# A two-layer decoder trunk on one core: layers written out, output projections and norms tile by tile, whole weight units, router with tokens as rows

## The chip, the cores and the metric

The kernel runs on one core of a Trainium2 chip, in one launch. The metric is device time in microseconds. A core has five engines with their own instruction streams, which meet only at semaphores: TensorE (PE; its weight loads are PEld), VectorE (DVE), ScalarE (ACT), GpSimd (POOL) and SyncE (SP). Here SP issues the weight loads and the output, POOL the other transfers.

## The reference, cut to what matters

One sequence of 256 tokens, width 1024, runs through two layers of three pre-norm residual parts. All tensors are float32.

```python
for layer in range(2):
    x = x + hybrid_mixer(rmsnorm(x, mix_norm_g[layer]), w_in, conv_w, pool_w, pool_scale, w_out, rel_bias)
    x = x + memory_cross_attention(rmsnorm(x, xattn_norm_g[layer]), mem_n, wq_x, wkv_x, wo_x)
    hn = rmsnorm(x, ffn_norm_g[layer])
    if layer == 0:                       # silu(hn @ w1) * (hn @ w3) @ w2, inner width 2816
        x = x + swiglu(hn, w13_dense, w2_dense)
    else:                                # top 2 of 8 experts, inner width 3584
        x = x + moe_swiglu(hn, router_w, w13_moe, w2_moe)
return rmsnorm(x, final_norm_g)
```

The mixer projects to 2560 columns: q, k, v of eight heads of 64, an input u of a causal pooling mixer (windows 2 to 16, mean less the token, then a small matrix per group), and b, c, h of a gated convolution of width 3 (b * conv(c * h)). The attention has a bias by distance, a 33-row table times a 0/1 matrix. Results of the three are joined and projected by w_out. Cross-attention has four heads of 128 over 256 memory tokens, whose norm is shared by both layers.

## The kernel before, in words

**Weights.** The host cuts all large weights into units of 128 x 2048 floats (1 MB), in the order of use, some of them half units (the projection wo_x, the last 256 columns of the dense stage). SP loads them in that order into a ring `raw` of six (`load`, L316). Each is split in two parts whose products PE can do in one pass each: ACT copies it to `w_hi` in a shorter format (`hi`, L460, in two halves; `hi_whole`, L468, for the expert items), DVE subtracts to get `w_lo` (`lo`, L707; `lo_whole`, L714). There are three slots of w_hi and w_lo. Activations are split in the same way (`xT_hi`, `xT_lo`; `yT_hi`, `yT_lo`). Each product is three matmuls (`passes`, L1104: high by high, high by low, low by high). `tokens_out` gives 128 tokens as rows, 512 columns at a time, for both row tiles t of 128 tokens; `features_out` gives features as rows, 256 tokens at a time. PE counts used halves in `unit_used`, DVE freed raw halves in `raw_free`; ACT, DVE, PE and SP wait on such counts.

**A norm** (`norm` on ACT L474, DVE L725, PE L1143): DVE squares and sums tile 0 while ACT does tile 1; ACT takes ln and exp(-ln/2) as a guess, DVE improves it by one Newton step, then scales both tiles with the gain row; PE transposes 16 blocks of 128 x 128 in four groups, and each group goes through ACT (`turned_hi`) and DVE (`turned_lo`). Between a projection and its norm stands `add_to_x` (L754), which adds the four 128 x 512 banks to x; the norm starts when all four are in.

**The order** of every engine's stream is written by hand. PE: the norm of x; the table product for the bias; then a hardware loop over two layers. In a layer: units 0 to 3 (q, k), 4 and 5 (v; in layer 0 the memory's norm between them), then ten iterations of attention (L1176 to 1208): iteration i does logits of head i, transposes of head i-1, values of head i-2, and in the first four also half a unit of features_out (units 6, 7). DVE adds the bias, takes the maximum and copies the transposes (L820 to 859), with units 8 to 10 split and the pooling in between; ACT does the exponentials. After it: unit 8, transposes of the attention's result, the pool matrices, unit 9, the output projection (units 10 to 13), memory keys (14, 15), norm, queries (17, 18) and memory values (16, 19), cross-attention (L1239 to 1273), projection by four half units, norm. Layer 0 goes on into the dense stage: five steps in a hardware loop and a rest of half width, with banks 4 to 7 cleared by four matmuls with zeros. Both loops, and the conditions on l, are run-time control flow on all engines.

**The bias table.** DVE copies the product's eight rows; POOL sends each row to memory 128 times (`skew`, L386), waits for it, and reads it back with one element less per partition, which lines up the distances (L399). DVE waits for that before the first head. The mem tile lies in the same buffer until its norm is done.

**The router** (L1345 to 1377): 16 matmuls with the router as stationary part give logits with experts as rows; a copy, two transposes and two steps on DVE turn and add them. DVE picks the top two, PE ranks the tokens of each expert, DVE builds a 0/1 matrix S, and PE gathers the first expert's rows by it. Then come the items, one for each expert, 42 units each (a hardware loop), and some for an overfull expert if any. At the end four indirect transfers bring the rows back, DVE adds them in, and the final norm follows.

The matmuls' waits on the low part of x at the start of a layer:

```python
            pe.wait_ge(sem("xT_lo"), l * 16 + 3)
            features_out(st, 0, 0, xs, (4, 5), True, False)
            pe.wait_ge(sem("xT_lo"), l * 16 + 4)
            features_out(st, 1, 4, xs, (4, 5), False, True)
```

## Time and profile before

| | |
|---|---|
| median of 3 runs (lowest, highest) | 1610.94 us (1609.52, 1611.62) |
| the profiled execution: its time / its span | 1611.02 us / 1609.1 us |
| mean granted TensorE clock | 0.962 |
| PE / PEld busy | 1499.7 / 1262.4 us |
| DVE / ACT / POOL busy | 1191.5 / 961.4 / 38.5 us |
| expert items, first to last matmul | about 633 to 1583 us |
| HBM read / written | 456.36 / 17.30 MB |

The profile is of one execution. Its span runs from the first to the last instruction. Busy time of PE says that matmuls were under way, not that they ran at full rate: the granted clock is 1.00 or 0.50 (2.4 or 1.2 GHz). Idle time is put down to what released the waiting engine.

### The profile page before, as it was taken

The page shows a single profiled execution, that of the slowest core. Times are in us where ns is not written, and L with a number is a line of the kernel's source. Part 1 is how long each engine was busy: PE and PEld are TensorE (multiplying, and loading weights), DVE is VectorE, ACT ScalarE, POOL GpSimd, SP SyncE. Part 2 cuts the span into 40 slices and gives each one's busy share as a digit, 9 for nine tenths or more (in the row PEclk, how much of TensorE's full clock was granted, in tenths as well). Part 3 has the DMA queues.
Part 4 walks back from the last instruction along what each step waited for, and adds up shares of the span by engine and source line. Part 5 has one row for each costly group of instructions (what it writes and reads, how often), then busy time and mean ns, then how long its engine had stood idle before and what let it go on. Part 6 is the DMA issues. An engine that isn't in the chain of part 4 may idle for free.

```text
span 1609.1 us, 22211 instructions
## 1 busy us (share of the span) xinstructions
PE 1499.7 (93%) x7397; PEld 1262.4 (78%) x7398; DVE 1191.5 (74%) x1027; ACT 961.4 (60%) x876; POOL 38.5 (2%) x53
## 2 busy tenths in 40 slices
PE   7699879999698986999999999999999999999993
PEld 6588767888687965888888888888888888888882
DVE  5467445454547646888888988898888888988884
ACT  4334334353334434777777777777777777777772
POOL 1000000000000000100000000000000000000001
PEclk9889989999898997999999999999999999999997
DMA  9524735435432422999999999999999999999992
GB/s 350 190 105 171 297 134 198 168 141 209 159 136 82 157 116 99 413 404 371 385 368 393 381 367 392 380 374 389 372 374 393 374 373 392 376 372 395 370 360 106
DMA packets 69723, 466.04 MB, mean 290 GB/s; under 512 B 7998, under 2 KB 8014, under 8 KB 17697
## 3 DMA queue, kind: packets, MB, share of 16 engines
q1 hardware_dynamic: 61328, 435.97, 69.9%
q0 software_dynamic: 8336, 29.34, 5.3%
q8 instruction: 31, 0.51, 0.1%
q14 instruction: 28, 0.22, 0.0%
HBM read 456.36 MB, written 17.30 MB: 294 GB/s over the span
## 4 chain that ended last, share of the span: by engine, by line
PE 89%; DMA 4%; DVE 4%; issue 2%; ACT 1%; DVEq 0%; POOLq 0%; POOL 0%; ACTq 0%
PE bank L1107 28%; PE bank L1109 27%; PE bank L1108 27%; DMA skew<-prob 3%; PE bank L1392 2%; PE bank L1149 1%; DMA bias<-skew 1%; PE bank L1381 0%; DVE xn L746 0%; PE bank L1271 0%; DVE w_lo L711 0%; PE bank L1371 0%; DMA probT<-done,row_i 0%; DVE w_lo L717 0%; PE bank L1251 0%
## 5 line engine op out<-in xcount | busy, mean ns | idle before, releaser
L717 DVE TENSOR_TENSOR w_lo<-raw,w_hi 128x2048 fp32r<-128x2048 f32 x336 | 769.0, 2292 | 103.1 <-ACT w_hi L471 99.9
L471 ACT ACTIVATE w_hi<-raw 128x2048 fp32r<-128x2048 f32 x336 | 642.9, 1916 | 126.3 <-PE bank L1109 126.3
L1107 PE MATMUL bank<-w_hi,yT_hi 128*128 128x512 f32 x1528 | 603.5, 395 | 6.4 <-DVE yT_lo L723 6.4
L1109 PE MATMUL bank<-w_hi,yT_lo 128*128 128x512 f32 x1528 | 596.8, 391 | 0.0
L1108 PE MATMUL bank<-w_lo,yT_hi 128*128 128x512 f32 x1528 | 595.9, 390 | 0.0
L1107 PEld LDWEIGHTS bank<-w_hi,yT_hi 128*128 128x128 f32 x1528 | 287.6, 188 | 66.9 <-issue 5.8
L1109 PEld LDWEIGHTS bank<-w_hi,yT_lo 128*128 128x128 f32 x1528 | 287.5, 188 | 61.0
L1108 PEld LDWEIGHTS bank<-w_lo,yT_hi 128*128 128x128 f32 x1528 | 288.0, 188 | 58.0
L711 DVE TENSOR_TENSOR w_lo<-raw,w_hi 128x1024 fp32r<-128x1024 f32 (+1 forms) x168 | 182.1, 1131 | 83.3 <-ACT w_hi L465 82.0
L465 ACT ACTIVATE w_hi<-raw 128x1024 fp32r<-128x1024 f32 (+1 forms) x168 | 155.8, 986 | 85.7 <-PE bank L1109 80.8
L723 DVE TENSOR_TENSOR yT_lo<-bank,yT_hi 128x512 fp32r<-128x512 f32 (+1 forms) x94 | 62.3, 678 | 59.1 <-ACT yT_hi L499 53.5
L1107 PE MATMUL bank<-xT_hi,w_hi 128*128 128x256 f32 x320 | 96.3, 301 | 6.9 <-DVE w_lo L711 6.9
L1108 PE MATMUL bank<-xT_lo,w_hi 128*128 128x256 f32 x320 | 94.5, 295 | 0.0
L1109 PE MATMUL bank<-xT_hi,w_lo 128*128 128x256 f32 x320 | 94.2, 294 | 0.0
L1107 PE MATMUL bank<-w_hi,xT_hi 128*128 128x512 f32 (+1 forms) x224 | 86.4, 386 | 6.9 <-DVE w_lo L711 6.8
L1109 PE MATMUL bank<-w_hi,xT_lo 128*128 128x512 f32 (+1 forms) x224 | 85.4, 381 | 0.0
L1108 PE MATMUL bank<-w_lo,xT_hi 128*128 128x512 f32 (+1 forms) x224 | 85.3, 381 | 0.0
L493 ACT ACTIVATE qk<-bank 128x512 f32<-128x512 f32 (+1 forms) x68 | 39.7, 592 | 75.8 <-PE bank L1109 75.8
L1107 PEld LDWEIGHTS bank<-xT_hi,w_hi 128*128 128x128 f32 x320 | 65.8, 206 | 10.2 <-DVE w_lo L711 8.7
L658 ACT ACTIVATE yT_hi<-bank 128x512 fp32r<-128x512 f32 x56 | 33.5, 599 | 59.2 <-PE bank L1392 59.2
L1108 PEld LDWEIGHTS bank<-xT_lo,w_hi 128*128 128x128 f32 x320 | 65.8, 206 | 0.1
L1109 PEld LDWEIGHTS bank<-xT_hi,w_lo 128*128 128x128 f32 x320 | 65.5, 205 | 0.0
(220 smaller groups left out, 919.4 us busy)
## 6 DMA issues: line engine op xcount, KB each, us to landing
raw<-in_moe_units SPq DMA_DIRECT2D x336, 1024.0 KB, 7.1
raw<-in_layer_units SPq DMA_DIRECT2D x40, 1024.0 KB, 6.7
raw<-in_dense_units SPq DMA_DIRECT2D x30, 1024.0 KB, 4.9
sent<-in_x POOLq DMA_DIRECT2D x1, 6144.0 KB, 33.3
xn<-sent POOLq DMA_DIRECT2D x9, 512.0 KB, 8.0
raw<-in_wo_units SPq DMA_DIRECT2D x8, 512.0 KB, 3.4
done<-qk POOLq DMA_DIRECT2D x8, 512.0 KB, 8.8
raw<-in_dense_halves SPq DMA_DIRECT2D x6, 512.0 KB, 3.2
```

The source lines that it names most:

```text
L465: act.activation(w_hi[:, u % SPLIT, half, 0:n], raw[:, u % RAW, half * n:(half + 1) * n], ACT.Copy)\
L471: act.activation(w_hi[:, u % SPLIT, :, :].rearrange("p a n -> p (a n)"), raw[:, u % RAW, :], ACT.Copy)\
L493: act.activation(hid[:, t, 0:width], bank[g_bank + t][:, 0:width], ACT.Silu)\
L658: act.activation(hT_hi[j % 2], banks4(3), ACT.Copy).then_inc(sem("hidT_hi"), 1)
L711: dve.tensor_tensor(w_lo[:, u % SPLIT, half, 0:n], raw[:, u % RAW, half * n:(half + 1) * n], w_hi[:, u % SPLIT, half, 0:n].bitcast(F32), A ...
L717: dve.tensor_tensor(w_lo[:, u % SPLIT, :, :].rearrange("p a n -> p (a n)"), raw[:, u % RAW, :], w_hi[:, u % SPLIT, :, :].rearrange("p a n ...
L723: return dve.tensor_tensor(out, src, hi_part.bitcast(F32), ALU.subtract)
L1107: pe.matmul(out, hi_l, hi_r, start=start, stop=False, skip_group_check=True)
L1108: pe.matmul(out, hi_l, lo_r, start=False, stop=False, skip_group_check=True)
L1109: return pe.matmul(out, lo_l, hi_r, start=False, stop=stop, skip_group_check=True)
L1149: mm = pe.transpose(bank[banks[2 * t + half]][:, k * P:(k + 1) * P], xn[:, t, a:a + P], ident)
L1392: mm = pe.transpose(bank[3][:, k * P:(k + 1) * P], hid[:, 0, k * P:(k + 1) * P], ident)
```

## The change

- Loops over the layers and over the dense steps are written out in Python: every engine's stream is straight code up to the items. `Stream` counts slots from an offset, so that a layer may have any number of units.
- All units are whole: 22 in a layer and 33 in the dense stage instead of 24 and 36. wo_x is two units, the dense rest three.
- The order of the input columns is v, q, k, (u, c), (h, b). The last seven halves of units 6 to 9 stand inside attention's iterations 0 to 6. u and c are copied by ACT to own buffers after head 2; pooling on DVE moves to iterations 3 and 4, the pool matrices to iteration 7. The output projection begins with its upper half (pooling, then convolution).
- Norms go tile by tile and half by half: ACT does all squares (two of 512 a tile), its `guess` and DVE's `root` are per tile. `project` finishes t0's sums before t1's; `norm_of_sum` on ACT and DVE works on t0 meanwhile, with splitting of the next units in between; `tile_by_tile` begins the next stage with t0.
- The dense stage's last units are ordered in the same way; the clearing matmuls go.
- In cross-attention the memory values' second unit (19) runs in iterations 0 and 1.
- x comes in two transfers, only the identity of `mats` from SP at the start. The skew table has 32 copies of a row instead of 128; SP issues it after unit 5, waits for it, and issues four reads of 32 partitions, then goes on with unit 6. The memory lies in qk's buffer.
- Router: x's parts are the stationary side, 16 matmuls for each tile, t0's before t1 is turned; the result has tokens as rows, and one reduction adds the parts.
- At the end rows come back tile by tile, and the final norm is per tile.

```diff
+LAYER_UNITS = 22
+DENSE_UNITS = 33
 ITEM_UNITS = 6 * (FE // FT)
 DENSE_STEPS = FD // FT
...
+    out += [unit(w_out, k, 4, c * 512, 512) for c, k in ((0, 4), (1, 4), (0, 0), (1, 0))]
     out += [unit(wkv, 4 * m, 4, 0, 512) for m in range(2)]
...
+                if l == 0 and u == RAW - 1:
+                    sp.wait_ge(sem("skew_rows"), 1)
+                    sp.dma_start(skew.ap(), skew_rows.unsqueeze(1).broadcast_to([HEADS, SKEW_P, SKEW_W]))\
+                        .then_inc(sem("skew_out"), 16)
+                    sp.wait_ge(sem("skew_out"), 16)
+                    for a in range(0, P, SKEW_P):
+                        sp.dma_start(bias[a:a + SKEW_P, :, :],
+                                     bass.AP(skew, P - 1 - a, [[SKEW_W - 1, SKEW_P], [SKEW_P * SKEW_W, HEADS], [1, T]]))\
+                            .then_inc(sem("bias_in"), 16)
...
-        pool.dma_start(skew.ap(), skew_rows.unsqueeze(1).broadcast_to([HEADS, P, SKEW_W])).then_inc(sem("skew_out"), 16)
...
+        def squares_of_sum(m, n, t, half):
+            act.wait_ge(sem("x_part"), 4 * n + 2 * t + half + 1)
+            square(m, t, half, x_tiles)
...
+        def guess(m, t):
+            act.wait_ge(sem("square"), 4 * m + 2 * t + 2)
+            act.wait_ge(sem("half_mean"), NT * m + t + 1)
+            act.activation(lnv[:, t:t + 1], ss[:, t, 1:2], ACT.Ln, scale=1.0 / D, bias=half_mean[:, t:t + 1])\
+                .then_inc(sem("ln_act"), 1)
+            act.wait_ge(sem("ln_act"), NT * m + t + 1)
+            act.activation(r0[:, t:t + 1], lnv[:, t:t + 1], ACT.Exp, scale=-0.5).then_inc(sem("rstd_guess"), 1)
...
+        def norm_of_sum(m, n, banks, st, u):
+            squares_of_sum(m, n, 0, 0)
+            squares_of_sum(m, n, 0, 1)
+            guess(m, 0)
+            hi(st, u, which=(0,))
+            squares_of_sum(m, n, 1, 0)
+            turned_hi(m, 0, banks[0:2], xT_hi)
+            hi(st, u, which=(1,))
+            squares_of_sum(m, n, 1, 1)
+            guess(m, 1)
+            hi(st, u + 1)
+            turned_hi(m, 1, banks[2:4], xT_hi)
...
+        def root(m, t):
+            a = slice(t, t + 1)
+            dve.wait_ge(sem("square"), 4 * m + 2 * t + 2)
+            dve.wait_ge(sem("half_mean"), NT * m + t + 1)
+            c.step(dve.tensor_scalar(mean[:, a], ss[:, t, 1:2], 1.0 / D, half_mean[:, a], ALU.mult, ALU.add))
+            dve.wait_ge(sem("rstd_guess"), NT * m + t + 1)
+            c.wait()
+            c.link(dve.scalar_tensor_tensor(newton[:, a], mean[:, a], r0[:, a], r0[:, a], ALU.mult, ALU.mult))
+            c.link(dve.tensor_scalar(newton[:, a], newton[:, a], -0.5, 1.5, ALU.mult, ALU.add))
+            c.link(dve.tensor_tensor(rstd[:, a], r0[:, a], newton[:, a], ALU.mult))
+        def scaled(m, t, src):
+            dve.wait_ge(sem("gain_in" if m else "first_gain_in"), 16 * m if m else 16)
+            for half in range(2):
+                s = slice(half * 512, (half + 1) * 512)
+                dve.scalar_tensor_tensor(xn[:, t, s], src[t][:, s], rstd[:, t:t + 1], g_row[:, s],
+                                         ALU.mult, ALU.mult).then_inc(sem("xn_ready"), 1)
...
+        def norm_of_sum(m, before, sums, banks, last, u, st):
+            dve.wait_ge(sem("sum_mm"), before + 1)
+            add_part(0, 0, sums[0])
+            half_means(m, 0)
+            dve.wait_ge(sem("sum_mm"), before + 2)
+            add_part(0, 1, sums[2])
+            root(m, 0)
+            scaled(m, 0, x_tiles)
+            if last[0] is None:
+                dve.wait_ge(sem("sum_mm"), before + 3)
             else:
...
+                used(dve, st, last[0])
+            add_part(1, 0, sums[1])
+            half_means(m, 1)
+            turned_lo(m, 0, banks[0:2], xT_hi, xT_lo)
+            used(dve, st, last[1])
+            add_part(1, 1, sums[3])
+            lo(st, u)
+            root(m, 1)
+            scaled(m, 1, x_tiles)
+            turned_lo(m, 1, banks[2:4], xT_hi, xT_lo)
+            lo(st, u + 1)
...
+                elif i == 3:
+                    dve.wait_ge(sem("u_sb"), l1)
+                    c.link(dve.tensor_tensor(B, U, pool_u[:, :, 1:T + 1], ALU.add))
...
                     c.link(dve.tensor_tensor(A[:, 1, :], B[:, 1, :], back(pool_b, 2)[:, 1, :], ALU.add))
...
+        def project(st, u, m, xs, sums, norm_banks):
             for t in range(NT):
...
+                for col in range(2):
+                    banks = sums[2 * col:2 * col + 2]
+                    first = u == 20
+                    if t == 0:
+                        tokens_out(st, u + col, 4, 512, xs, banks, first, True, tiles=(t,), count=False)\
+                            .then_inc(sem("sum_mm"), 1)
+                    elif col == 0:
+                        tokens_out(st, u, 4, 512, xs, banks, first, True, tiles=(t,))
+                    else:
+                        tokens_out(st, u + 1, 4, 512, xs, banks, first, True, which=(0,), tiles=(t,))
+                        turn_tile(m, 0, norm_banks[0:2])
+                        tokens_out(st, u + 1, 4, 512, xs, banks, first, True, which=(1,), tiles=(t,))
...
+        def tile_by_tile(st, u, m, banks, norm_banks):
+            lower, upper = (xT_hi, xT_lo, 0), (xT_hi, xT_lo, 4)
+            turned(m, 0, 0)
+            tokens_out(st, u, 4, 512, lower, banks, True, False, tiles=(0,), count=False)
+            turned(m, 0, 1)
+            tokens_out(st, u + 1, 4, 512, upper, banks, False, True, which=(0,), tiles=(0,), count=False)
+            if m:
+                turn_tile(m, 1, norm_banks[2:4])
+            tokens_out(st, u + 1, 4, 512, upper, banks, False, True, which=(1,), tiles=(0,), count=False)
+            turned(m, 1, 0)
+            tokens_out(st, u, 4, 512, lower, banks, True, False, tiles=(1,))
+            turned(m, 1, 1)
+            tokens_out(st, u + 1, 4, 512, upper, banks, False, True, tiles=(1,))
         pe.sem_inc(sem("unit_used"), 2 * SPLIT)
...
+            tile_by_tile(st, 0, 4 * l, (0, 1), (0, 1, 2, 3))
+            features_out(st, 2, 0, xs, (4, 5), True, False)
+            features_out(st, 3, 4, xs, (4, 5), False, True)
+            if l < 1:
+                pe.wait_ge(sem("skew_rows"), 1)
+                turn_tile(1, 0, (2, 3))
...
+                if i == 3:
+                    pe.wait_ge(sem("u_sb"), l1)
+                    pe.wait_ge(sem("c_sb"), l1)
+                if i < 7:
+                    u = 6 + (i + 1) // 2
+                    features_out(st, u, 4 * (u % 2), xs, (2, 3), u % 2 == 0, u % 2 == 1, which=((i + 1) % 2,))
+                if i == 7:
...
+            pe.wait_ge(sem("pool_lo"), l1 * 2)
+            tokens_out(st, 10, 4, 512, (yT_hi, yT_lo, 4), (0, 1), True, False, which=(0,))
+            tokens_out(st, 11, 4, 512, (yT_hi, yT_lo, 4), (6, 7), True, False, which=(0,))
             for t in range(NT):
                 pe.wait_ge(sem("y_tok"), l * 2 + t + 1)
                 for k in range(4):
                     mm = pe.transpose(bank[4 + t][:, k * P:(k + 1) * P], y_tok[:, t, k * P:(k + 1) * P], ident)
                 mm.then_inc(sem("yTok_mm"), 1)
...
+            pe.wait_ge(sem("conv_lo"), l1)
+            tokens_out(st, 10, 4, 512, (yT_hi, yT_lo, 4), (0, 1), False, False, which=(1,))
+            tokens_out(st, 11, 4, 512, (yT_hi, yT_lo, 4), (6, 7), False, False, which=(1,))
+            pe.wait_ge(sem("attn_lo"), l1 * NT)
+            m = 3 * l + 2
+            project(st, 12, m, (yT_hi, yT_lo, 0), (0, 1, 6, 7), (2, 3, 4, 5))
             ms = (memT_hi, memT_lo)
...
                 turn(FT // 2, NT)
+                down(st, e + 3, 1, tiles=(0,), count=False)
                 pe.wait_ge(sem("hidT_lo"), (DENSE_STEPS + 1) * NT)
...
+                down_short(st, e + 4, 0, 0)
+                down_short(st, e + 4, 0, 1)
+                down(st, e + 3, 1, tiles=(1,))
+                down_short(st, e + 4, 1, 0)
+                turn_tile(4, 0, (0, 1))
+                down_short(st, e + 4, 1, 1)
+        m = 3 * DEPTH
...
+        for t in range(NT):
+            turned(m, t, 1)
+            for k in range(KD):
+                for part in (xT_hi, xT_lo):
+                    mm = pe.matmul(bank[0][:, t * 2 * NE:(t + 1) * 2 * NE], part[:, k, t * P:(t + 1) * P],
+                                   router_parts[:, k, :], start=(k == 0 and part is xT_hi),
+                                   stop=(k == KD - 1 and part is xT_lo))
+            if t == 0:
+                turn_tile(m, 1, (6, 7))
         mm.then_inc(sem("router_mm"), 1)
```

## Rows read from the trace of the kernel before

**Rows 1.** The page, busy time of each engine (share of the span).

```profile
PE 1499.7 (93%) x7397; PEld 1262.4 (78%) x7398; DVE 1191.5 (74%) x1027; ACT 961.4 (60%) x876; POOL 38.5 (2%) x53
```

**Rows 2.** Windows: length; busy us of PE, PEld, DVE, ACT, POOL; granted clock, DMA share, GB/s.

```profile
0.00:633.00 633.00, 549.86 (x3077) 477.73 (x3078) 337.93 (x523) 249.69 (x394) 16.80 (x28) 0.92 0.47 172
...
633.00:1583.00 950.00, 949.81 (x4320) 784.64 (x4320) 843.98 (x493) 707.68 (x475) 17.31 (x20) 1.00 0.96 372
```

**Rows 3.** Waits of PE before 700 us: who waits for whom, total us, times, longest.

```profile
PE bank L1149 <- DVE xn L746: 27.5, 4, 9.9
PE bank L1197 <- ACT prob L533: 18.0, 8, 12.1
PE bank L1107 <- DVE w_lo L711: 13.8, 4, 5.2
PE bank L1107 <- DVE yT_lo L723: 6.4, 4, 1.8
PE bank L1352 <- issue: 4.6, 1, 4.6
PE bank L1260 <- ACT prob L580: 3.6, 4, 1.2
```

**Rows 4.** Timeline at the start: start us, us, instruction, [idle before <- releaser].

```profile
16.70 0.58 PE L1107 MATMUL bank<-xT_hi,w_hi 128*128 128x256 f32 x1 [1.77 <-DVE w_lo L711]
```

**Rows 5.** First attention transpose (timeline); DMA issues: count, KB, us to landing.

```profile
72.73 0.69 PE L1197 MATMUL bank<-mats,prob 128*128 128x128 f32 x2 [12.11 <-ACT prob L533]
...
skew<-prob POOLq DMA_DIRECT2D x1, 1536.0 KB, 40.4
...
bias<-skew POOLq DMA_DIRECT2D x1, 1024.0 KB, 14.0
```

**Rows 6.** Timeline of PE, attention of layer 1: heads 3, 4, 5, and the last.

```profile
477.12 0.49 PE L1185 MATMUL bank<-qk 64*128 64x128 f32 x2
...
482.00 0.48 PE L1185 MATMUL bank<-qk 64*128 64x128 f32 x2
...
483.94 0.48 PE L1185 MATMUL bank<-qk 64*128 64x128 f32 x2
...
498.41 0.63 PE L1205 MATMUL bank<-v,probT 128*128 128x64 f32 x2
```

**Rows 7.** Windows at the lower clock.

```profile
72.70:76.70 4.00, 3.97 (x19) 3.97 (x20) 0.56 (x1) 2.80 (x6) 0.00 (x0) 0.50 0.03 8
...
218.30:223.60 5.30, 5.30 (x13) 4.19 (x14) 5.30 (x5) 3.38 (x4) 0.00 (x0) 0.50 0.59 193
428.60:431.80 3.20, 3.20 (x15) 3.20 (x16) 3.20 (x3) 3.20 (x4) 0.00 (x0) 0.50 0.26 41
...
498.80:503.50 4.70, 4.70 (x24) 4.70 (x24) 2.37 (x4) 0.00 (x0) 0.00 (x0) 0.50 0.51 185
```

**Rows 8.** Windows over three norms, the last with the router.

```profile
205.20:218.30 13.10, 3.32 (x17) 3.09 (x17) 9.81 (x17) 7.62 (x12) 0.58 (x1) 0.81 0.13 41
413.10:428.60 15.50, 3.69 (x17) 3.27 (x16) 11.12 (x19) 6.40 (x11) 2.84 (x4) 0.66 0.16 43
600.20:633.20 33.00, 15.65 (x78) 13.39 (x77) 21.20 (x47) 12.36 (x16) 0.53 (x1) 0.64 0.32 113
```

**Rows 9.** The page, the splitting of half units: count, busy us, mean ns, idle before.

```profile
L711 DVE TENSOR_TENSOR w_lo<-raw,w_hi 128x1024 fp32r<-128x1024 f32 (+1 forms) x168 | 182.1, 1131 | 83.3 <-ACT w_hi L465 82.0
L465 ACT ACTIVATE w_hi<-raw 128x1024 fp32r<-128x1024 f32 (+1 forms) x168 | 155.8, 986 | 85.7 <-PE bank L1109 80.8
```

**Rows 10.** Timeline of DVE, norm before the dense stage: adding halves, scaling tiles.

```profile
205.20 1.29 DVE L762 TENSOR_TENSOR x<-x,bank 128x512 f32<-128x512 f32 x2 [4.15 <-PE bank L1109]
...
209.29 2.48 DVE L746 SCALAR_TENSOR_TENSOR xn<-x,rstd,g_row 128x1024 f32<-128x1024 f32 x2
```

**Rows 11.** DMA queues, instruction fetches: in 245:400 (a loop), 433:600 (straight code).

```profile
q8 instruction: 3, 0.05, 0.1%
...
q8 instruction: 8, 0.13, 0.3%
```

More of the change, by code:

```diff
@@ L572, in _ @@
[L572 to L574 removed]
+            hi(st, 20)
+            if l == DEPTH - 1:
+                act.wait_ge(sem("router_in"), 32)
+                act.activation(router_parts[:, :, 0:NE], router[:, :, :], ACT.Copy).then_inc(sem("router_hi"), 1)
             for h in range(XHEADS):
@@ L1341, in _ @@
                 pe.wait_ge(sem("hidT_lo"), (DENSE_STEPS + 1) * NT)
-                down(st, e + 6, NT, short=True, last=True)
-                norm(4, (0, 1, 2, 3))
-            pe.nop()
-        pe.wait_ge(sem("xT_lo"), 16 * DEPTH - 4)
-        pe.wait_ge(sem("router_lo"), 1)
-        for k in range(KD):
-            for part in (xT_hi, xT_lo):
-                mm = pe.matmul(bank[0][0:2 * NE, 0:T], router_parts[:, k, :], part[:, k, :],
-                               start=(k == 0 and part is xT_hi), stop=(k == KD - 1 and part is xT_lo))
```

784 lines of the change are left out of this document (360 added, 424 removed).

## The prediction, on record before the changed kernel was run

> **What bounds the kernel now.** I read the page first. PE is busy 93% of the span [rows 1], so gains can only come from the rest and from low clock. The windows split that: from 633 to 1583 us, the expert items, PE is busy 949.8 of 950 us at clock 1.00; before it, 549.9 of 633 us at clock 0.92 [rows 2]. The diff leaves the item loop alone (only slot numbers shift, as it starts at unit 77 instead of 84), and DMA, though at share 0.96, never makes PE wait there. So everything hangs on the first 633 us and the 26 us behind the items. The list of PE's waits names the places [rows 3]: transposes wait for the scaled rows of a norm (27.5 us in 4), attention transposes for the exponentials (18.0, of which 12.1 in one), first matmuls of a stage for w_lo (13.8) or for the low part of the activations (6.4). The windows on the lower clock show a second price behind each [rows 7]: half speed for 3 to 5 us after work resumes. A microsecond of full-speed PE work done at clock 0.50 costs a second one.
>
> **The change part by part.** The matmuls are the same in number and shape nearly everywhere, so I work with removed and added gaps. All durations are of the one profiled execution: span 1609.1 us, its time 1611.02, 0.1 above the median 1610.94.
>
> *1. Start.* The first matmul is at 16.70 us [rows 4]. x now comes in two tiles, and unit 0 is split before the second tile is turned. By my count ACT and DVE are still in the way: the squares of a tile are now two on ACT, and both tiles' scaling stands ahead of the first w_lo. First matmul at about 14.7, but at half speed at first. I take 1.5 us of gain; between 0 and 4.
>
> *2. Bias table.* PE stands 12.11 us before the first attention transpose [rows 5]: the skewed table took 40.4 us out and 14.0 us back. Then 4 us run at clock 0.50 [rows 7], costing 2. Now 32 copies of each row go out instead of 128: a quarter of 1536 KB, so at the old rate 10 us. Its source is still 8 partitions. It is issued by SP behind unit 5 once DVE has copied the rows, which now stands behind the splitting of units 0 and 1, about 20.4 us. Behind the six megabytes already in SP's queue it starts near 25 (1 MB passes in 2.8 us at 372 GB/s [rows 2]), ends near 35; the bias follows in four parts, at most the old 14: 49. Attention wants it at about 57 (72.7 less 12.1, less the 1.5 of step 1, less the head's own 2 us). So the wait goes, with its clock loss: 14.1. While SP waits for the skew table it issues no weights: unit 6 is asked for at about 36 and lands by 41 to 52; PE reaches it at about 55. Bounds 0 and 14.1.
>
> Here a rule speaks against the change. In rows 5 the table on its own queue took 40.4 us next to the weights. The Trainium skill (DMA: Bandwidth & Descriptors, Queues, rings and completion order) says that on each DMA engine the descriptors of a ring are consumed in order, while different rings are served in turn. By it the table no longer shares with the weights but waits for all six. That is the start at 25 used above, against 20.4 without the rule; the step keeps 8 us of slack either way, less in rival A.
>
> *3. Attention.* Iterations with half a unit of projection beside them last 4.88 us, those without 1.94 [rows 6]. In the old order only four of ten have filler. From 483.94 (head 5) to the end at about 498.8 the work is three iterations of 1.94 and the tails of two (1.1, 0.7), 7.6 us; it took 14.9. Lost 7.3, and 4.7 us at clock 0.50 behind it cost 2.3 more [rows 7]. That is 9.6; the waits for ACT prob beyond the 12.1, 5.9 us, lie about evenly in both layers, so I take 8.7 for layer 0 (less of it at the lower clock): together 18.3. Now iterations 0 to 6 have filler, and pool matmuls stand in the seventh. DVE per iteration: about 1.6 us of softmax and copy, and 2 x 1.13 for a unit [rows 9] or some 3 for pooling: inside 4.88. New: before the upper half of the output projection PE waits for the convolution (products, y_tok, taps, half of unit 12, its low part, some 7.7 us of DVE against 5.4 + 0.9 of PE): 1.4 us, once a layer. Net 18.3 - 3.0 = 15.3; bounds 8 and 18.
>
> *4. Norm behind the mixer's projection.* It was hidden behind the memory keys (no wait of it in the list). It stays behind them, but DVE now has one more chain: add, half unit pair, root, scaling before the second tile turns, 5.3 us against 5.7 of PE. I charge 1.0; bounds 0 and 4 of loss.
>
> *5. Cross-attention.* Unit 19 (values) moves into its first two iterations. The exponential's wait, 3.6 us in 4 [rows 3], loses its two longer parts: 2.4. Splitting of w_lo leaves the path between y_tok and the projection: 0.5 a layer. 3.4; bounds 0 and 5.
>
> *6. Norm before the dense stage.* From the last projection matmul to the first of the dense stage: 13.1 us [rows 8], then 5.3 us at 0.50, 2.7 lost [rows 7]. New order: with t0's sum 5.4 us ahead of t1's, its chain (add 0.65, two scalings of half a tile 1.3 [rows 10], and between them the square, logarithm, exponential and root, which the old order does in 2.8 from add to scaling for both tiles and I put at 2.4: 4.4) ends when PE has 1.4 us of projection left. Counting on from there: transposes 1.8, a wait of 0.3 for the scaling, 0.7 for the first low part, 1.0 for the second tile's scaling, which stands behind both halves of a w_lo: 3.8 in all instead of 15.8. Gain 12.0; bounds 7 and 13. The 2.5 us wait near 246 stays; the four clearing matmuls that go were inside it.
>
> *7. Layer boundary.* 15.5 us [rows 8], 3.2 us at 0.50 behind it (1.6) [rows 7], and 1.3 of the waits for yT_lo, which the last full down unit now covers. t1 follows t0 by two short and one full pass, so the new cost is again about 3.6. Gain 14.8; bounds 9 and 15.
>
> *8. Norm and router.* 33.0 us from the end of the projection to the first item [rows 8]. 4.6 of it PE waits for nothing the profile shows [rows 3]; about 2.9 of that lie after the last operand is ready. New: t0's 16 router matmuls run while t1 is normed; logits come out with tokens as rows, so a copy, two transposes and a copy (2.2 us) go. With the old stretch's durations, all inside those 33.0: end of projection to last xT_lo 8.1 + the interleaved transposes' 1.1, router 1.8, top-2 2.8, ranks 2.2, S 0.9, gather 5.6, its split 1.5: 24.0, and 0.5 for the hand-overs. Gain 8.5; bounds 4 (32 small matmuls, each with a full weight load, at half clock) and 12.
>
> *9. Tail.* The final norm runs on the same engines as the one of rows 10. Tile by tile, the squares of t1 now stand behind the root of t0 on ACT, whose half mean stands behind all four combinings on DVE. The second tile ends 0.3 later. -0.3; bounds -1 and 1.
>
> *10. Allowance.* New short waits stand close together at each norm; the clock dropped in such places before. Three windows of 3.4 us at half rate: -5. Bounds 0 and -10.
>
> Sum: 1.5 + 14.1 + 15.3 - 1.0 + 3.4 + 12.0 + 14.8 + 8.5 - 0.3 - 5.0 = 63.3 us. Span 1545.8, time 1547.7, less the 0.1: **1547.6 us**.
>
> **Rivals.**
> *A. The skew table blocks the weights.* If on SP's queue it still needs about 40 us (few source partitions), bias lands near 75 and unit 6 behind it: step 2 turns from +14.1 to -13. Saving 36, 1575 us. For: 40.4 us in rows 5. Against: a quarter of the bytes, and weights no longer beside it. 0.12.
> *B. Per-tile norms are longer than counted.* Each is a chain over three engines with single-column steps, and sits behind w_lo work in DVE's order. If each of the three big norms exposes 5 us more, and the convolution wait is 3 instead of 1.4: 1547.6 + 15 + 3 = 1566. For: rows 8, where 13 us were exposed. Against: nothing in the count is longer than its row. 0.15.
> *C. Instruction supply (ends slower).* Written-out layers and dense steps are straight code: PE's fetches in the dense stretch were 3 in a loop against 8 in as long a stretch of straight code [rows 11]. If a fetch stalled PE as at the router (2.9 us), 22 stalls eat the gain; with 25 or more, time is above 1611, say 1620. Against: those 8 fetches left no such wait in rows 3. 0.03.
> *D. More than counted.* Loop ends may cost beyond the router's. The Trainium skill (Runtime: NRT & Kernel Launch, Instruction fetch mechanics) says that a taken branch to code outside the fetched window stalls. By it the dense loop's turns would each pay, and writing it out would bring some 2.9 us at each of four turns, about 1536 us. This trace disagrees inside the loop: no wait there but 2.5 us for w_lo. 0.07.
>
> **How the numbers follow.** Forecast 0.63, own range 1536 to 1560; A 0.12, B 0.15, C 0.03, D 0.07. Range 1534 to 1574 holds the forecast, B, D and the nearer part of A. A change under 0.2% (3.2 us) can't be told from none here. All but C are faster by far more: faster 0.96, same 0.01, slower 0.03.
>
> **What would show it.** Right: no wait of ten us for ACT prob in layer 0; bias landed before 50 us; norm waits under 2 us each; items beginning near 570 instead of 633 and again 950 us long. Wrong: a DVE wait for the bias, PE waits on "issue", a clock of 0.50 in long stretches of the layers, or a longer item loop.

## The result, and the profile after

The changed kernel takes 1546.81 us (median of 4 runs, 1543.76 to 1548.75), the kernel before 1611.22 (4 runs, 1609.52 to 1611.62): ratio 0.96, 95% interval 0.9581 to 0.962. Forecast: 1547.6. The profiled execution took 1543.76 us, its span is 1541.9, 67.2 less than before; the forecast had 63.3 less.

The page's first rows of the kernel after stand beside [rows 1]; the clock's row shows one dip in 40 slices, the last slice aside.

```profile
PE 1479.3 (96%) x7408; PEld 1244.0 (81%) x7408; DVE 1187.9 (77%) x1052; ACT 973.6 (63%) x928; POOL 35.8 (2%) x53
...
PEclk9999999999999979999999999999999999999996
```

Windows of the kernel after, columns as in [rows 2]: what lies ahead of the items, then the items.

```profile
0.00:564.00 564.00, 529.24 (x3088) 459.18 (x3088) 334.43 (x543) 259.89 (x438) 15.61 (x28) 0.98 0.52 191
564.00:1514.00 950.00, 949.77 (x4320) 784.79 (x4320) 843.94 (x493) 707.77 (x475) 15.82 (x20) 1.00 0.96 372
```

The items are as long as before, 950 us. Everything was won ahead of them: 633 us became 564, with 20.6 us less of PE busy time (549.9 against 529.2) because less of it ran at half clock (0.92 to 0.98), and 48 us less idle. The end behind the items gave 1.5 us back. Waits of PE before 640 us in the kernel after, to be read against [rows 3]:

```profile
PE bank L1190 <- DVE xn L774: 14.0, 5, 9.4
PE bank L1147 <- DVE yT_lo L750: 5.1, 5, 1.5
PE bank L1147 <- DVE w_lo L738: 4.9, 4, 3.5
PE bank L1448 <- DVE mask L1043: 2.9, 1, 2.9
PE bank L1440 <- DVE xT_lo L750: 2.5, 2, 1.4
```

Of the 14.0 us for scaled rows 9.4 are the first wait of the kernel, for x; the four later ones together are 4.6, where there were 17.6 behind the first 9.9. Attention's waits for ACT prob, 18.0 in [rows 3], left this list; 0.4 us for the convolution stands there instead, in each layer. Timelines of the kernel after at its norms (start, length, instruction, idle before it): ahead of the dense stage, then at the layer boundary.

```profile
183.84 1.32 PE L1190 MATMUL bank<-mats,xn 128*128 128x128 f32 x8 [0.70 <-DVE xn L774]
...
372.81 1.32 PE L1190 MATMUL bank<-mats,xn 128*128 128x128 f32 x8 [0.69 <-DVE xn L774]
376.04 0.50 PE L1147 MATMUL bank<-w_hi,xT_hi 128*128 128x512 f32 x1 [0.52 <-DVE xT_lo L750]
```

Where 13.1 and 15.5 us stood [rows 8] there are pauses of 0.4 to 0.7 us. What is left above 2 us behind the start, by the timeline of PE, is one wait in the dense stage and two in the router:

```profile
206.34 0.73 PE L1147 MATMUL bank<-w_hi,xT_hi 128*128 128x512 f32 x1 [3.47 <-DVE w_lo L738]
...
543.41 1.97 PE L1190 MATMUL bank<-mats,xn 128*128 128x128 f32 x8 [2.47 <-DVE xn L774]
...
553.31 0.57 PE L1448 MATMUL bank<-mask,mats 128*128 128x8 f32 x2 [2.94 <-DVE mask L1043]
```

The low clock went with the waits, except here. Windows of the kernel after, against [rows 7] (which show a part of what there was: 99 us at 0.50 before the items, now 24):

```profile
206.40:209.80 3.40, 3.40 (x8) 2.71 (x9) 3.20 (x3) 1.37 (x2) 0.00 (x0) 0.50 0.26 43
...
540.90:561.40 20.50, 12.63 (x57) 12.03 (x57) 10.55 (x33) 5.05 (x7) 0.53 (x1) 0.50 0.34 128
```

### The profile page after: what moved, and what is told of

The parts are those of the page before. It is cut to its first block, busy times and chain, and to the rows that moved or that the text cites. A ratio compares the mean times of both kernels' runs of the same rounds, so it can differ in the third digit from the quotient of the medians.

```text
span 1541.9 us, 21452 instructions
## 1 busy us (share of the span) xinstructions
PE 1479.3 (96%) x7408; PEld 1244.0 (81%) x7408; DVE 1187.9 (77%) x1052; ACT 973.6 (63%) x928; POOL 35.8 (2%) x53
## 4 chain that ended last, share of the span: by engine, by line
PE 91%; DVE 5%; issue 1%; ACT 1%; DMA 1%; POOLq 0%; POOL 0%; ACTq 0%; DVEq 0%; SPq 0%
PE bank L1147 28%; PE bank L1149 28%; PE bank L1148 28%; PE bank L1479 2%; DVE w_lo L738 1%; DVE xn L774 1%; PE bank L1190 1%; PE bank L1264 0%; PE bank L1331 0%; PE bank L1274 0%; DMA g_row<-in_mix_norm_g 0%; PE bank L1262 0%; PE bank L1468 0%; PE bank L1351 0%; PE bank L1458 0%
## 5 line engine op out<-in xcount | busy, mean ns | idle before, releaser
L738 DVE TENSOR_TENSOR w_lo<-raw,w_hi 128x1024 fp32r<-128x1024 f32 x160 | 188.4, 1220 | 56.4 <-ACT w_hi L468 54.8
L468 ACT ACTIVATE w_hi<-raw 128x1024 fp32r<-128x1024 f32 x160 | 160.5, 1055 | 39.5 <-PE bank L1149 37.3
L1147 PE MATMUL bank<-xT_hi,w_hi 128*128 128x256 f32 x320 | 91.8, 287 | 0.0
L1148 PE MATMUL bank<-xT_lo,w_hi 128*128 128x256 f32 x320 | 90.5, 283 | 0.0
L1149 PE MATMUL bank<-xT_hi,w_lo 128*128 128x256 f32 x320 | 90.4, 283 | 0.0
L682 ACT ACTIVATE yT_hi<-bank 128x512 fp32r<-128x512 f32 x56 | 33.6, 599 | 59.3 <-PE bank L1479 59.3
L1147 PEld LDWEIGHTS bank<-xT_hi,w_hi 128*128 128x128 f32 x320 | 61.3, 192 | 0.7 <-DVE w_lo L738 0.7
L1148 PEld LDWEIGHTS bank<-xT_lo,w_hi 128*128 128x128 f32 x320 | 61.3, 192 | 0.1
L1149 PEld LDWEIGHTS bank<-xT_hi,w_lo 128*128 128x128 f32 x320 | 61.3, 191 | 0.0
```

The costliest lines, as they stand in the source:

```text
L468: act.activation(w_hi[:, st.split(u), half, :], raw[:, st.slot(u), half * n:(half + 1) * n], ACT.Copy)\
L682: act.activation(hT_hi[j % 2], banks4(3), ACT.Copy).then_inc(sem("hidT_hi"), 1)
L738: dve.tensor_tensor(w_lo[:, st.split(u), half, :], raw[:, st.slot(u), half * n:(half + 1) * n], w_hi[:, st.split(u), half, :].bitcast(F32) ...
L1147: pe.matmul(out, hi_l, hi_r, start=start, stop=False, skip_group_check=True)
L1148: pe.matmul(out, hi_l, lo_r, start=False, stop=False, skip_group_check=True)
L1149: return pe.matmul(out, lo_l, hi_r, start=False, stop=stop, skip_group_check=True)
```

## The experiments

Eleven variants ran, and the kernel after once more. The times of the kernel before in their runs lie between 1611.1 and 1612.1 us (medians); gains are worked out from the ratio to it, which for the kernel after is 0.96, and in its second set of runs 0.9583: its own median moved by 2.4 us between the two sets (1546.81 and 1544.43), so differences under about 3 us between variants of the kernel after are read from stages of the profile, not from the times.

**The bias table: what made it late.** First in the kernel after, the number of copies put back to 128, still written by SP:

```diff
-SKEW_W, SKEW_P = 384, 32
+SKEW_W, SKEW_P = 384, 128
```

> The changed kernel with 128 copies of each table row again (one read-back instead of four), still issued by SP between unit 5 and unit 6. Theory (the table and the units share SP's ring, in order, and SP issues no units meanwhile): the table of 384 KB needed 13.9 us from issue at 20.1 us; with four times the bytes it ends near 60 us, the bias near 68, unit 6 lands after that; PE reaches unit 6 at 52.6 us and stands until about 70: 17 to 22 us slower than the changed kernel, near 1566 us. Rival (SP's queue moves the table much faster than POOL's did, the copies' number is not what counts): under 5 us slower.

Measured: 1562.52 us (1561.61 to 1563.89), ratio 0.9696 [0.9679, 0.9712], 15.7 above the kernel after: the theory's mechanism, a little under its 17 to 22 us. In SP's timeline the table was issued at 19.35 us and the bias and the next weights at 58 (kernel with 128 copies); in the kernel after they follow at 34:

```profile
58.15 0.40 SPq L344 DMA_DIRECT2D bias<-skew  x1
58.67 3.17 SPq L326 DMA_DIRECT2D raw<-in_layer_units  x6
```

```profile
20.12 0.87 SPq L340 DMA_DIRECT2D skew<-probT  x1
33.97 1.82 SPq L344 DMA_DIRECT2D bias<-skew  x4
35.90 2.30 SPq L326 DMA_DIRECT2D raw<-in_layer_units  x5
```

And PE, by its waits in the kernel with 128 copies, waits for weights, not for the bias:

```profile
PE bank L1147 <- DVE w_lo L738: 20.6, 5, 15.7
```

So rival A's mechanism is real: SP stands behind the table and the weights stand behind SP. It lost because the quarter of the bytes took 13.9 us from issue to landing, not 40.

What those 13.9 us are made of, the counts of DMA packets tell. The table's packets are rows of 1536 bytes, 32 copies of 8 rows, so 256 of them, and nothing else that moves here lies between 512 bytes and 2 KB. The kernel after from the table's issue to 27.8 us, then from 27.8 to its landing:

```profile
DMA packets 593, 2.89 MB, mean 376 GB/s; under 512 B 158, under 2 KB 158, under 8 KB 323
```

```profile
DMA packets 304, 0.58 MB, mean 99 GB/s; under 512 B 26, under 2 KB 282, under 8 KB 282
```

Not one packet of the table moved in the first 7.7 us, while the six weight units ahead of it in SP's queue passed; then all 256 moved within 5.9. With 128 copies it is the same: none from 19.3 to 27.6 us, then 30 us for the 1024.

Then the same question from the other side, in the kernel before: 32 copies alone, all on GpSimd's queue as it was.

```diff
-    skew = nc.dram_tensor("skew", [HEADS, P, SKEW_W], F32, kind="Internal")
+    skew = nc.dram_tensor("skew", [HEADS, SKEW_P, SKEW_W], F32, kind="Internal")
...
+                for a in range(0, P, SKEW_P):
+                    pool.dma_start(bias[a:a + SKEW_P, :, :],
+                                   bass.AP(skew, P - 1 - a, [[SKEW_W - 1, SKEW_P], [SKEW_P * SKEW_W, HEADS], [1, T]]))\
+                        .then_inc(sem("bias_in"), 16)
```

> The kernel before with one edit of the change alone: the table is written to memory in 32 copies, not 128, and read back in four pieces; both stay on GpSimd's queue behind its other transfers. Theory: the size of the write was what made the first head's exp late, not the queue: the write takes about 14 us, not 38, the wait of 12.11 us for ACT prob at layer 0 goes to under 1 us, with part of the stretch at a clock of 0.50 behind it (62.9 to 78.2 us): 12 to 15 us faster than before, the 13.3 us that a difference of stages gave for this step in the after kernel. Rival: GpSimd's queue and the other transfers set the landing; the wait shrinks by less than half and under 6 us are gained.

Measured: 1604.24 us (1602.34 to 1605.01), ratio 0.9948 [0.9934, 0.9962]: 8.4 us, between theory (12 to 15) and rival (under 6). The timeline of GpSimd's queue in that kernel tells why:

```profile
15.81 0.74 POOL L386 DMA_DIRECT2D skew<-prob  x1 [3.48 <-DVE prob L792]
...
48.96 0.58 POOL L373 DMA_DIRECT2D g_row<-in_xattn_norm_g  x1 [30.11 <-DVE xn L748]
49.53 2.34 POOL L400 DMA_DIRECT2D bias<-skew  x4
```

The table had landed 14.3 us after its issue, at 30, but the read stands in GpSimd's order behind a gain that waits for the norm of mem, and so until 49; PE's wait shrank from 12.11 to 4.54 us. It could not simply be put ahead: mem lay in the buffer that the bias goes to. The last kernel moves both, mem and the read:

```diff
-    mem_sb = bias[:, :, :].rearrange("p h c -> p (h c)").rearrange("p (t d) -> p t d", t=NT)
+    class MemTiles:
+        def __getitem__(self, key):
+            _, t, cols = key
+            return prob[:, :, :].rearrange("p t c -> p (t c)")[:, cols] if t == 0 else v[:, :, :].rearrange("p t c -> p (t c)")[:, cols]
+    mem_sb = MemTiles()
...
-            load_gain(l * 3 + 2, io["xattn_norm_g"][l])
             if l == 0:
                 pool.wait_ge(sem("skew_out"), 16)
                 for a in range(0, P, SKEW_P):
...
+            load_gain(l * 3 + 2, io["xattn_norm_g"][l])
```

> The kernel before with 32 copies of the table (as in the run with 32 copies, 8.4 us faster by the ratio) and the other half of the step: the bias is read back right behind the write, ahead of the cross-attention's gain, for which GpSimd waited until 48.96 us. For that mem no longer lies where the bias goes: its two tiles are loaded into buffers of probabilities and values. Theory: the rest of the wait at layer 0 (4.54 us of 12.11 for ACT prob, and the low clock behind it) was this place in GpSimd's queue; the bias lands before 45 us, no wait over 1.2 us is left at the heads of layer 0, and the whole step comes to 12 to 15 us: 1597 to 1600. Rival: the rest is no matter of the table, and the time is that of the 32 copies alone, 1604.

Measured: 1597.16 us (1596.64 to 1597.9), ratio 0.991 [0.9893, 0.9926]: 14.5 us, of which the place is 6.1 by the ratios (7.1 by the medians, from 1604.24). The edit also moves the table's rows and splits mem's load in two, which the place needed. GpSimd's queue and PE's wait in that kernel:

```profile
30.39 2.34 POOL L404 DMA_DIRECT2D bias<-skew  x4 [11.83 <-DMA skew<-probT]
```

```profile
PE bank L1205 <- ACT prob L541: 4.1, 6, 1.1
```

The step is thus settled without SP's queue: 8.4 us come with fewer bytes and about 6 more with the earlier place. The order matters: in the kernel before the table landed at about 56 us, and the gain stood only until 49.10, so an earlier place alone would have gained nothing. The diff's move of mem out of the bias's buffer is what lets the read go early.

**Attention's order.** In the kernel after, the last four halves of projection behind the heads, not between them:

```diff
-                if i < 7:
+                if i < 3:
...
+            for i in range(3, 7):
+                u = 6 + (i + 1) // 2
+                features_out(st, u, 4 * (u % 2), xs, (2, 3), u % 2 == 0, u % 2 == 1, which=((i + 1) % 2,))
```

> The changed kernel with only three half units inside attention's iterations (0 to 2) and the other four between attention and the output projection, as many beside attention as before. Theory (half units hide the chain over DVE and ACT, and keep the clock up): the loss of the old order comes back, 7 to 9 us a layer, 14 to 18 us slower than the changed kernel, with windows of clock 0.50 at the end of each attention. Rival (the gain of that stage came from pooling and the output projection's upper half being moved): under 6 us slower.

Measured: 1562.25 us (1561.36 to 1564.13), ratio 0.9689 [0.9673, 0.9705], 15.4 above the kernel after. By its waits and its windows:

```profile
PE bank L1274 <- ACT prob L567: 6.0, 6, 2.1
```

```profile
77.00:94.10 17.10, 15.00 (x65) 12.71 (x65) 7.04 (x22) 2.98 (x13) 0.00 (x0) 0.50 0.18 62
445.60:462.70 17.10, 16.09 (x69) 13.22 (x68) 8.27 (x24) 4.27 (x14) 0.00 (x0) 0.50 0.19 62
```

Six short waits are 6 us. The 31.1 us of PE work in the two stretches at 0.50 would take half at full clock where nothing else holds it. That is an estimate of at most 15.5 us; with the 6 it is more than the 15.4 measured, so part of the one hides behind the other. No run here filled these waits, so how the 15.4 divide is argued, not shown.

**Loops written out, alone.** The kernel before with its layers and dense steps written out on every engine, nothing else:

```diff
-        with pe.Fori(0, DEPTH) as l:
+        for l in range(DEPTH):
...
-                with pe.Fori(1, DENSE_STEPS) as j:
+                for j in range(1, DENSE_STEPS):
```

> The kernel before with its loops over layers and dense steps and the conditions on the layer written out, nothing else. Theory: only the wait of 2.9 us before the router goes, and perhaps 1 to 2 us at the turn of the layers: 2 to 5 us faster than before, about 1607. Rival D: each turn of the dense loop cost too, 10 us or more faster. Rival C: straight code costs fetches, slower than before.

Measured: 1608.86 us (1608.02 to 1611.5), ratio 0.9985 [0.9975, 0.9994], 2.4 us by the ratio, 3.1 by the medians. Waits of PE:

```profile
PE bank L1357 <- DVE probT L987: 4.5, 1, 4.5
...
PE bank L1352 <- DVE router_parts L723: 1.6, 1, 1.6
```

The 4.6 us on "issue" at the router [rows 3] went, but 1.6 of them stayed at the same instruction as a wait for VectorE, and 2.8 came back one wait later (1.7 to 4.5), behind weight splits that stand ahead in VectorE's order. So the router's stage gained nothing: from the first transpose of its norm to the first item 28.5 us pass (603.77 to 632.27), where it was 27.5 (605.71 to 633.17). What was gained lies at the turn of the layers, where the wait for w_lo is 2.98 us instead of 5.17. (This profile is of an execution of 1611.05 us; its first item begins 0.9 us earlier than before, so it shows less than the medians.) A turn of the dense loop takes 33.56 us in the kernel before (from transposes at 253.37 to those at 286.93), 33.55 written out here and 33.57 in the kernel after. Fetches between 245 and 400 us rose from 3 [rows 11] to 6 without a wait. Neither C nor D.

**The projection's order.** In the kernel after, both tiles' sums per column half again, and the norm behind them:

```diff
-            for t in range(NT):
-                for col in range(2):
+            for col in range(2):
+                banks = sums[2 * col:2 * col + 2]
+                tokens_out(st, u + col, 4, 512, xs, banks, first, True, tiles=(0,), count=False)\
+                    .then_inc(sem("sum_mm"), 1)
+                tokens_out(st, u + col, 4, 512, xs, banks, first, True, tiles=(1,))
+            turn_tile(m, 0, norm_banks[0:2])
```

> The changed kernel with each attention output projection in the old order, both tiles' sums for one column half, then for the other, and tile 0 turned behind it. The dense stage's end is left as changed. Theory (the lead of tile 0's sums hides the norm's chain): t0's second sum comes 2.7 us later and nothing of the projection is left to cover its scaling; about 2.5 us more wait at the two exposed norms (dense stage, router) and 1.6 at the two mixer norms, 6 to 10 us slower than the changed kernel. Rival (what hides the chain is only the work behind it): under 2 us.

Measured: 1557.57 us (1555.43 to 1558.92), ratio 0.9665 [0.9649, 0.9681], 10.8 above the kernel after, just over the theory's range. The waits for scaled rows grew by 2.9 us only:

```profile
PE bank L1190 <- DVE xn L774: 16.9, 10, 8.9
```

That is far less than the loss. PE's waits for low parts of x grew by 3.0 us beside them (2.5 to 4.0 at the router's matmuls, 0.9 to 2.4 ahead of the next stage), and the profile shows two new stretches at 0.50 (169.8 to 173.2, 186.8 to 190.2 us) with 6.8 us of PE work, which cost up to 3.4. The three together are 9.3 of the 11.7 us by which the profiled spans differ; the rest is open.

**How much of the norms' price was clock.** In the kernel before, TensorE multiplies zeros while it waits. This shortens no wait:

```diff
+        def idle(b, n):
+            for _ in range(n):
+                pe.matmul(bank[b][:, :], zeros[:, 0:P], zeros[:, :], start=True, stop=True, skip_group_check=True)
...
+            idle(4, 22)
             norm(l * 3 + 3, (4, 5, 6, 7))
+            idle(0, 16)
```

> The kernel before, with TensorE kept busy while it waits for the norms ahead of the dense stage, of layer 1 and of the router: independent 128x512 products of a tile of zeros (bf16) into banks that nobody reads, 22 to 26 ahead of the transposes and 16 to 20 behind them, and 6, 12 and 3 at the router's waits. No wait for a norm is shortened and nothing is moved, so this separates the clock's part of what the after kernel gained there from the wait's part. Theory: the waits themselves (5.46 and 4.35, 6.64 and 5.17, 5.47 and 4.57 us) stay, but the stretches at a granted clock of 0.50 behind them (210.0 to 213.4 and 216.8 to 223.6, 418.2 to 431.8, 602.5 to 609.3 and 612.7 to 629.8 us, with 28.6 us of TensorE busy time in them) go; at twice the clock half of that busy time is saved, less where VectorE sets the pace: 9 to 14 us faster than before, granted clock up from 0.962 to about 0.98. Rival 1: the low clock has nothing to do with TensorE's idleness at the norms: same time, same 0.50 stretches. Rival 2: the products outlast the waits and delay the transposes: up to 3 us of the gain is lost again.

Measured: 1601.81 us (1599.06 to 1603.25), ratio 0.9937 [0.9923, 0.995]: 10.1 us. Windows over the three norms of that kernel:

```profile
196.30:223.60 27.30, 25.45 (x117) 17.49 (x119) 17.66 (x26) 13.97 (x19) 0.58 (x1) 0.99 0.31 105
400.00:430.00 30.00, 25.39 (x144) 17.74 (x146) 19.21 (x28) 13.79 (x21) 2.84 (x4) 1.00 0.32 105
590.00:630.00 40.00, 33.68 (x183) 22.61 (x185) 27.48 (x76) 15.63 (x18) 1.61 (x2) 1.00 0.29 105
```

The transposes begin 5.5 us after the end of the last projection matmul (205.48 to 210.96), as before (5.47), and the clock is 0.99 to 1.00 where it was 0.81, 0.66 and 0.64 [rows 8]. 10 of the 33.1 us that the three norms' steps brought could be had by the clock alone.

**What is left: the dense step.** In the kernel after, units 4 and 5 split ahead of silu and gate:

```diff
-                lo(st, 3)
+                for u in range(3, 6):
+                    lo(st, u)
                 gate_tiles(FT, NT, 0)
```

> The after kernel with one order changed: in the first dense step units 4 and 5 are split by ScalarE and VectorE ahead of silu and gate, not behind them. Theory: TensorE's wait of 3.47 us at 202.87 us (for w_lo, second dense step) goes, and with it the stretch at a clock of 0.50 at 206.4 to 209.8 us (1.7 us): 4 to 5 us faster than the after kernel, that is 64 + 4.5 us faster than before, about 1542. Rival: gate and silu now come later and the wait turns up at the transposes of the hidden tile instead (they stand 5.1 us of TensorE work later): under 1 us gained.

Measured: 1545.11 us (1543.45 to 1546.62), ratio 0.9586 [0.9573, 0.96]: no difference that the times can tell. The wait for w_lo went, and in its place PE waits for the gate, by the list of waits:

```profile
PE bank L1151 <- DVE qk L820: 2.0, 1, 2.0
```

3.47 became 2.01, and a stretch of 3.4 us at 0.50 stands behind it as before (208.6 to 212.0 us): mostly the rival, at another instruction than it named.

**The router's norm ahead of the splits.** Two splits moved behind the scaling on VectorE:

```diff
-            lo(st, u)
+            if m < 3 * DEPTH:
+                lo(st, u)
             root(m, 1)
             scaled(m, 1, x_tiles)
```

> The after kernel with one order changed on VectorE in the router's norm: the weight splits (2.35 us, standing at 539.4 us ahead of the second tile's root) come behind its scaling, and the next unit's split behind the selection matrix. Theory: TensorE's wait of 2.46 us for xn shrinks to about 0.4, and the stretch keeps its low clock: 2 to 3 us faster than the after kernel. Rival: the clock sets this stretch and the wait moves on to the next tile's parts or to the mask: under 1 us.

Measured: 1546.48 us (1542.3 to 1546.87), ratio 0.959 [0.9577, 0.9603]: again nothing in the time. In the timeline the wait of 2.47 us is 1.32, not the 0.4 expected, and from the router's first matmul to the first item 23.6 us pass instead of 25.2:

```profile
546.21 1.12 PE L1197 MATMUL bank<-mats,xn 128*128 128x128 f32 x4 [1.32 <-DVE xn L774]
```

**The router's waits filled.** In the kernel after, products of 512 columns in the six waits:

```diff
+        idle(6, 4)
         for t in range(NT):
             turned(m, t, 1)
...
         mm.then_inc(sem("router_mm"), 1)
+        idle(4, 11)
```

> The after kernel with TensorE kept busy at the six waits of the router (538 to 564 us): 4, 4, 5, 11, 3 and 5 independent 128x512 products of split activations into a bank that nobody reads. Order and waits are unchanged. Theory: the stretch of 20.5 us at a granted clock of 0.50 (540.9 to 561.4 us), in which TensorE is busy for about 14 us, runs at full clock, and half the busy time is saved: 4 to 7 us faster than the after kernel. Rival: the stretch is slow because the router's own matmuls have 16 columns; the low clock stays and the added products cost up to 3 us.

Measured: 1539.11 us (1538.06 to 1546.15), ratio 0.9568 [0.9547, 0.9588]. The times alone overlap; the stage does not: the first item begins at 559.45 us instead of 564.23. The router's own matmuls still have 16 columns and run at 1.00, so the rival is out. A window over the router of that kernel:

```profile
537.50:562.00 24.50, 21.58 (x130) 17.34 (x129) 17.27 (x54) 9.10 (x17) 0.53 (x1) 1.00 0.29 107
```

**All of it, and the kernel after again.** Beside the three above: the first dense step's left half in banks 4 and 5, so that the next step doesn't wait for the gate; the waits behind cross-attention filled; the last norm's first mean ahead of the last combination.

```diff
-                tile_by_tile(st, 0, 3, (0, 1), (4, 5, 6, 7))
+                tile_by_tile(st, 0, 3, (4, 5), (4, 5, 6, 7))
...
+                    if j > 1:
                         pe.wait_ge(sem("hid_ready"), j * NT)
```

> The after kernel with everything that the runs so far point to: router's waits filled; its norm ahead of the weight splits; dense units 4 and 5 split ahead of silu; the first dense step's left half collected in banks 4 and 5, so that the second step need not wait for the gate (the wait that took the place of w_lo); the waits behind cross-attention filled with 3 and 5 products that nobody reads; the last norm's first mean ahead of the last combination. Theory: the gains add: 7.7 for the fill, 1.5 for the norm's order, 4 to 5 for the dense step (3.47 us of wait and 1.7 us of clock), 0.5 at the end: 1533 us (1530 to 1537), with no stretch at 0.50 between 30 us and the router's end. Rival: waits move on as they did with units 4 and 5 alone, and only the fill counts: 1537 to 1540 us.

> The after kernel unchanged, as the reference for small differences: 1547 us (1543 to 1549). Where its profile shows a stretch at 0.50 near 166 us or not, it tells whether that stretch belongs to an edit or comes and goes by itself.

Measured: all together 1534.62 us (1533.4 to 1535.42), ratio 0.9519 [0.9506, 0.9532]; the kernel after in the same runs 1544.43 (1543.0 to 1548.48), ratio 0.9583 [0.957, 0.9596]. So 9.8 us faster than the changed kernel. The combined kernel's page and its longest waits (9.4 us of the first row is the wait for x at the start):

```profile
PEclk9999999999999999999999999999999999999996
```

```profile
PE bank L1204 <- DVE xn L776: 11.9, 5, 9.4
PE bank L1161 <- DVE yT_lo L752: 1.7, 5, 0.4
PE bank L1161 <- DVE w_lo L740: 1.4, 3, 0.6
```

One of its numbers missed: a stretch of 3.4 us at 0.50 remains, near 549 us. And the kernel after, run again, has a low stretch near 167 us that its first profile did not have, and the one near 207 is twice as long as the 3.4 us there:

```profile
166.60:170.00 3.40, 3.15 (x8) 2.55 (x9) 2.46 (x3) 0.00 (x0) 0.00 (x0) 0.52 0.00 0
207.40:210.80 3.40, 2.47 (x6) 2.02 (x7) 3.40 (x4) 2.36 (x3) 0.00 (x0) 0.51 0.08 12
210.80:214.20 3.40, 3.40 (x9) 2.63 (x9) 0.79 (x1) 0.00 (x0) 0.00 (x0) 0.50 0.88 340
```

Its first item begins at 568.06 us, 3.8 later than in the first profile of the same kernel. That is the scatter in which the two edits above drowned, both with such a stretch near 167 us in their profiles.

## Why the prediction held, step by step

Stage points with equal work on both sides of them, in the two profiles, each of one execution. In brackets what was forecast.

- *1, start*: first attention logits at 55.54 instead of 55.80 us, with 2.87 us more work done by then: +3.1 (+1.5). Full clock is reached at about 18.5 us instead of 22; I had counted the first matmul alone (15.19, forecast 14.7).
- *2, bias table*: +13.3 by difference of the two layers, +14.5 in the kernel before by itself (+14.1). Bias landed at about 40 us, forecast 49. The size was right, the picture incomplete: I credited the bytes and SP's queue, and did not see that the read would next be held by its place behind a gain, and mem by its buffer. The table's own path was forecast well: its packets moved from 27.9 to 33.6 us, forecast 25 to 35. The rule of the Trainium skill that the prediction weighed (DMA: Bandwidth & Descriptors, Queues, rings and completion order) agrees with this trace: the table waited 7.8 us for the six weight units ahead of it in SP's queue. It did not decide anything, because the 5.8 us that followed were short: 13.9 from issue to landing, against 14.3 on GpSimd's own queue beside the weights.
- *3 and 4, attention and the mixer's norm*: +16.1 (+15.3 - 1.0). The convolution's wait is 0.4 us a layer, not 1.4 (and two of 1.4 are 2.8, where the sum took 3.0). Fewer halves between the heads bring the loss back, 15.4 us for both layers.
- *5, cross-attention*: +3.1 (+3.4).
- *6, norm before the dense stage*: +13.8 (+12.0), 1.7 of it a low stretch near 193 us that went and that I had not listed.
- *7, layer boundary*: +12.1 (+14.8). The pauses there are 1.9 us; the rest of the miss lies in the dense steps behind the first: small new waits for w_lo (0.60 at one place) and the low stretch at 206 us.
- *8, norm and router*: +7.2 (+8.5). The order was counted rightly, at full clock. The stretch runs at 0.50 for 20.5 us, and filling its waits gives 4.8 us back: the low bound's cause (small matmuls at half clock) happened to half of the 32. The sum also took 2.9 us from the 4.6 on "issue"; the loops written out alone show that this went into later waits.
- *9, tail*: -1.5 (-0.3): ScalarE starts its last copy 1.7 us after the last matmul, where it followed at once. The profile names nothing that it waited for.
- *10, allowance for new clock drops*: 0 (-5.0) beyond what is booked above. The drops came, but at the router (4.8 us in step 8) and near 206 us (1.7 in step 7), 6.5 together; the pauses of 0.4 to 1.4 us elsewhere did not lower the clock in the first profile. In the second a stretch near 167 us did, and its first item came 3.8 us later in all.

The sum is 67.2. It was 3.9 above the forecast because of steps 1, 3, 6 and 10, less 7 to 9 and a little of 2 and 5. The waits that went are the ones that the prediction named, but that the median lies only 0.8 us from the forecast is partly luck: the misses of the single steps add up to 16.5 us and cancel, and the profile is of the fastest of the four executions. Of the signs that the prediction named, one did not hold: the norm wait at the router is 2.47 us, not under 2, with 20.5 us at 0.50 around it. A's mechanism was seen once its bytes were put back; B's 5 us per norm did not come (0.4 to 0.9 each), and putting the projection's old order back costs 10.8 us in all; C and D were taken out by the loops written out alone, 2.4 to 3.1 us. The Trainium skill (Runtime: NRT & Kernel Launch, Instruction fetch mechanics) has a taken branch stall where its target isn't in the fetched window. No turn of the dense loop stalled (33.56 us in the loop, 33.55 written out), and no trace here tells whether their targets lay outside it, so rival D is out without the rule being tested.

## What to carry to other kernels

Price a wait with what it does to TensorE's clock behind it: at the three norms about a third of the gain (10.1 of 33.1 us) was to be had from the clock alone. Where a wait can't be removed, products that nobody reads keep the clock up, at no cost if they end before the wait does. For a late transfer look for its bytes, for its place in the issuing engine's order and for the buffer that it must wait for: here mending one exposed the next. When a wait goes, look at once for the next instruction that the engine would wait for; two of the edits here (the loops written out, at the router, and the dense units ahead of silu) moved a wait more than they removed it.

## What the runs showed of the hardware

- Multiplying zeros in bf16 holds the granted clock at 1.00 through waits that otherwise end in 3.4 to 17.1 us at 0.50: 10.1 us for 143 products.
- The same program has a low stretch in one execution and not in the next, behind the same pauses of 0.71, 0.85 and 1.41 us; the first item begins at 564.23 and at 568.06 us.
- The table, written from 8 partitions, takes 13.9 to 14.3 us for 384 KB and 38.8 to 40.4 us for 1536 KB from issue to landing (58.15 less 19.35, and [rows 5]). On SP's queue the first 8 us of that are the wait for the weights ahead; its packets then pass in 5.8 and 30.1 us, 68 and 52 GB/s, where the weights of the items move at 372 [rows 2].
- 6 instruction fetches instead of 3 in 155 us of straight code cost nothing that shows, and neither does the turn of a hardware loop: 33.56 us for each of the dense steps in the loop, 33.55 written out.
